# A fourth place for split weights, low splits behind the norms, and a first gate/up step by tile in a four-layer fp32 decoder

## The reference

```python
for i in range(2):                                  # L0, L1
    q, k, v = project_qkv(x, w_qkv[i], cos, sin)    # 16 query heads, 4 key heads of 64, partial rope
    a = moba_attention(q, k, v) if i == 0 else sliding_window_attention(q, k, v, sinks)
    x = layer_norm(alpha * x + a @ w_o[i], ...)
    f = (swiglu(x, w_ffn_gate, w_ffn_up, w_ffn_down) if i == 0        # d_ff 3584
         else moe_swiglu(x, w_router, w_gate, w_up, w_down))         # 8 experts of 3584, top 2
    x = layer_norm(alpha * x + f, ...)
    x = x + (p[i] @ w_ple_proj[i]) * sigmoid(x @ w_ple_gate[i])
for l in range(2):                                  # L2, L3
    h = hybrid_mixer(rmsnorm(x, pre_mix_norm[l]), ...)   # gated delta rule and dilated attention
    x = x + rmsnorm(h, post_mix_norm[l])
    u = causal_conv3(rmsnorm(x, pre_ffn_norm[l]) @ ffn_up[l]) + bias  # 2 x 2816 columns
    x = x + rmsnorm((gelu(gate) * val) @ ffn_down[l], post_ffn_norm[l])
```

## Time and profile before

| | us |
|---|---|
| median of 3 runs | 2222.71 (2221.61 to 2225.2) |
| the profiled execution | 2222.56 |
| its span | 2220.8 |
| TensorE busy | 2165.2 |
| VectorE busy | 1740.5 |
| ScalarE busy | 1423.9 |

### The profile page before, as it was taken

The page is one execution under the profiler, slowest core; times in us unless marked ns, Lnnn a source line. Parts: engine busy times, 40 slices in busy tenths (PEclk is TensorE's granted clock), DMA queues, the critical chain, the costliest instruction groups (busy, mean ns, idle before and its releaser), DMA issues.

```text
span 2220.8 us, 30779 instructions
## 1 busy us (share of the span) xinstructions
PE 2165.2 (97%) x11356; PEld 1808.8 (81%) x11356; DVE 1740.5 (78%) x2003; ACT 1423.9 (64%) x1581; POOL 54.9 (2%) x72
## 2 busy tenths in 40 slices
PE   9999999989999999999999999989999999999998
PEld 6688897668888888888888887779978898987888
DVE  7765567688888888888888889767667886776886
ACT  6544434657877777777777776656565556565654
POOL 2000000010000000000000003000000000000000
PEclk9999999999999999999999999999999999999999
DMA  9755554269999999999999999843135454224551
GB/s 387 261 190 190 190 184 178 105 238 388 367 389 369 393 371 383 371 387 377 366 388 372 386 362 385 338 170 137 67 139 193 177 202 151 81 105 152 190 187 60
DMA packets 83234, 573.25 MB, mean 258 GB/s; under 512 B 9712, under 2 KB 10336, under 8 KB 17936
## 3 DMA queue, kind: packets, MB, share of 16 engines
q1 hardware_dynamic: 77472, 545.29, 64.6%
q0 software_dynamic: 5376, 26.12, 3.2%
q10 hardware_dynamic: 288, 0.52, 0.1%
HBM read 564.03 MB, written 17.83 MB: 262 GB/s over the span
## 4 chain that ended last, share of the span: by engine, by line
PE 85%; DVE 7%; ACT 4%; issue 2%; DMA 1%; SPq 0%; ACTq 0%; DVEq 0%
PE bank L800 63%; PE bank L866 10%; PE bank L868 5%; DVE w_lo L538 2%; ACT w_hi L533 2%; PE bank L1150 1%; PE bank L1275 1%; PE bank L1285 1%; DVE R L2023 1%; PE bank L1190 1%; DVE arena L2034 1%; ACT arena L1483 1%; DMA raw<-in_wu_qkv 1%; ACT L533 0%; PE bank L921 0%
## 5 line engine op out<-in xcount | busy, mean ns | idle before, releaser
L538 DVE TENSOR_TENSOR w_lo<-raw,w_hi 128x2048 fp32r<-128x2048 f32 x505 | 1156.4, 2300 | 263.5 <-ACT w_hi L533 261.8
L533 ACT CAST w_hi<-raw 128x2048 fp32r<-128x2048 f32 x505 | 963.8, 1912 | 351.0 <-PE bank L800 261.3
L800 PE MATMUL bank<-w_hi,xT 128*128 128x512 f32 x2368 | 754.9, 393 | 10.5 <-DVE xT L1978 4.2
L800 PEld LDWEIGHTS bank<-w_hi,xT 128*128 128x128 f32 x2368 | 445.4, 188 | 116.0 <-DVE w_lo L538 11.8
L800 PE MATMUL bank<-w_lo,xT 128*128 128x512 f32 x1184 | 462.0, 390 | 0.0
L800 PE MATMUL bank<-w_hi,aT_hi 128*128 128x512 f32 x864 | 344.0, 398 | 2.4 <-DVE w_lo L538 2.4
L866 PE MATMUL bank<-xT,w_hi 128*128 128x512 f32 x960 | 341.1, 399 | 4.1 <-DVE xT L1978 2.9
L800 PE MATMUL bank<-w_hi,aT_lo 128*128 128x512 f32 x864 | 337.4, 390 | 0.0
L800 PE MATMUL bank<-w_lo,aT_hi 128*128 128x512 f32 x864 | 336.5, 389 | 0.0
L868 PE MATMUL bank<-xT,w_lo 128*128 128x256 f32 x960 | 269.9, 281 | 0.0
L800 PEld LDWEIGHTS bank<-w_lo,xT 128*128 128x128 f32 x1184 | 222.8, 188 | 44.1 <-issue 0.5
(11 more groups left out here) (340 smaller groups left out, 1697.3 us busy)
## 6 DMA issues: line engine op xcount, KB each, us to landing
raw<-in_wu_eg SPq DMA_DIRECT2D x112, 1024.0 KB, 7.2
raw<-in_wu_eu SPq DMA_DIRECT2D x112, 1024.0 KB, 7.2
raw<-in_wu_ed SPq DMA_DIRECT2D x112, 1024.0 KB, 7.3
raw<-in_wu_up SPq DMA_DIRECT2D x44, 1024.0 KB, 4.8
raw<-in_wu_ffn_gu SPq DMA_DIRECT2D x28, 1024.0 KB, 4.8
raw<-in_wu_in SPq DMA_DIRECT2D x28, 1024.0 KB, 4.9
raw<-in_wu_down SPq DMA_DIRECT2D x22, 1024.0 KB, 4.8
raw<-in_wu_ffn_d SPq DMA_DIRECT2D x14, 1024.0 KB, 4.8
```

The costliest lines, as they stand in the source:

```text
L533: nc.scalar.copy(w_hi[:, place(i), :], src).then_inc(*E.hi.mark("unit", i))
L538: nc.vector.tensor_tensor(w_lo[:, place(i), :], raw[:, i % RAW, :], w_hi[:, place(i), :].bitcast(F32), ALU.subtract) \
L800: mm = nc.tensor.matmul(o, l[i], r[j], start=(first and n == 0), stop=(last and n == 2), skip_group_check=not lone)
```

## The change

Outside the experts there are DEEP = 4 places for split units and 4 raw slots; a `walk` there splits the unit four further on. In the experts `vec` and `X` are the fifth and sixth raw slot, so the load into the fifth waits for the tokens' last use of the vectors and the sixth for the dispatch; GpSimd loads the vectors 6 and 7 after the loop. The start of L0 splits unit 3 alone, and the next one ahead of the keys' rope. Low splits that stood ahead of norms stand behind them. In L0, L2 and L3 the first gate/up step is made of `first_high(L, 0)` between the turns of the tiles, `first_high(L, 1)` and `first_low(L)`, and the turned tiles stand in banks 0 to 3.

```diff
-WARM_START, WARM_LN, WARM_RMS = 4, 4, 4
+WARM_START, WARM_LN, WARM_RMS = 4, 4, 2
 RAW = 6
+RAW_OUT = 4
+RAW_OVF = 3
 SPLIT = 3
+DEEP = 4
...
+        raw = [raw_out[:, s, :] for s in range(RAW_OUT)] + [a[:, :, :].rearrange("p a b -> p (a b)") for a in (vec, X)]
+        high = [w_hi[:, s, :] for s in range(DEEP)]
+        low = [w_lo[:, s, :] for s in range(DEEP)]
...
-            return (4 if stage[1] == "mix" else 0) + 2 * t + g
+            return 2 * g + t if stage[1] == "mix" else 2 * t + g
...
+            if base is None:
+                no = split_units.index(i) + DEEP
+                if no < len(split_units) and not i < expert_base <= split_units[no]:
+                    split(E, eng, split_units[no])
+            elif E is M or i + SPLIT < TURN:
+                split(E, eng, i + SPLIT)
...
+                                if j < RAW_OUT:
+                                    sp.wait_ge(*at_once(M.lo, "unit", expert_base - RAW_OUT + j))
+                                if j == RAW_OUT:
+                                    sp.wait_ge(*x_ready.at(1, "mix", 1))
+                                if j == RAW_OUT + 1:
+                                    sp.wait_ge(*xg_put.at("all"))
+                                    sp.wait_ge(*at_once(M.act, "scaled"))
+                                    sp.wait_ge(*at_once(M.groups, "moe", "first", "ga", 1))
...
+                gp.wait_ge(*M.lo.at("unit", expert_base + TURN - 1))
+                load_vec(6)
+                load_vec(7)
...
+            def first_high(L, t):
+
+                for i in range(2):
+                    n = unit_at["gu", L, 0, i]
+                    tile_ready((L, "mix"), t, (i,))
+                    pe.wait_ge(*M.hi.at("unit", key_of(n)))
+                    for half in range(2):
+                        for m in range(2):
+                            b = 4 + 2 * half + m
+                            o = open_bank(M, b) if i == 0 and t == 0 else bank[b]
+                            both = o[:, :].rearrange("p (a n) -> p a n", a=2)[:, :, t * P:(t + 1) * P]
+                            for kc in range(4 * i, 4 * i + 4):
+                                c0 = (kc % 4) * 512 + half * 256 + m * P
+                                nc.tensor.matmul(both, high[place(n)][:, c0:c0 + P], x_both[:, :, kc, t * P:(t + 1) * P],
+                                                 start=(kc == 0 and t == 0), stop=False, skip_group_check=True)
+
+            def first_low(L):
+
+                for i in range(2):
+                    key = ("gu", L, 0, i)
+                    u = unit(M, pe, key)
+                    for half in range(2):
+                        for m in range(2):
+                            for kc in range(4 * i, 4 * i + 4):
+                                c0 = (kc % 4) * 512 + half * 256 + m * P
+                                mm = nc.tensor.matmul(bank[4 + 2 * half + m][:, S:2 * S], u[1][:, c0:c0 + P], xT[0][:, kc, :],
+                                                      start=False, stop=(kc == KC - 1), skip_group_check=True)
+                        if i == 1:
+                            mm.then_inc(*M.groups.mark("gu", L, 0, half))
+                    name = ("gu", L, 0, 1) if i else ("unit",) + key
+                    if i == 0:
+                        mm.then_inc(*M.groups.mark(*name))
+                    released(M, unit_at[key], *name)
...
-                    if s < n - 2:
-                        features(L, s, None if s else (L, "mix"))
+                    if s == 0:
+                        first_high(L, 1)
+                        first_low(L)
+                    elif s < n - 2:
+                        features(L, s)
                     else:
                         o = [open_bank(M, 4 + 2 * (s % 2) + half) for half in range(2)]
...
-                keep_warm(WARM_LN, 6)
+                if L == 0:
+                    first_high(L, 0)
+                else:
+                    keep_warm(WARM_LN, 6)
...
-                keep_warm(WARM_RMS, turn_bank((L, "mix"), 1, 0))
+                keep_warm(WARM_RMS, 6)
+                first_high(L, 0)
                 enter("mix", 1)
...
-                if L:
-                    walk("qkv", L, 4)
+                walk("qkv", L, 4)
                 block(2, 4)
...
-            walk("qkv", 0, 4)
+            nc.scalar.copy(high[place(2)][:, half:UNIT], raw[2][:, half:UNIT]).then_inc(*M.hi.mark("unit", 2))
...
-                walk("wo", L, 0)
-                walk("wo", L, 2)
+                if L == 0:
+                    walk("wo", L, 0)
+                    walk("wo", L, 2)
+                else:
+                    for i in range(2):
+                        split_hi(M, ac, expert_base + i)
                 norm_root(L, "mix", 0)
-                walk("wo", L, 1)
+                if L == 0:
+                    walk("wo", L, 1)
                 copy_T((L, "mix"), L, 0)
-                walk("wo", L, 3)
+                if L == 0:
+                    walk("wo", L, 3)
                 norm_root(L, "mix", 1)
                 copy_T((L, "mix"), L, 1)
                 if L == 0:
...
                 walk("wo", L, 0)
                 want_root()
                 half_squares(L, "mix", 0, wo_halves)
+                sum_squares(L, "pre", 0, x_ready.at(L, "mix", 0))
                 walk("wo", L, 2)
-                sum_squares(L, "pre", 0, x_ready.at(L, "mix", 0))
                 walk("wo", L, 1)
                 half_squares(L, "mix", 1, wo_halves)
+                copy_T((L, "mix"), L, 0)
                 sum_squares(L, "pre", 1, x_ready.at(L, "mix", 1))
-                for t in range(NT):
-                    copy_T((L, "mix"), L, t)
+                copy_T((L, "mix"), L, 1)
                 walk("wo", L, 3)
                 dense_act(L)
                 n = FFN_STEPS[L]
...
-                walk("wo", L, 0)
+                if L == 0:
+                    walk("wo", L, 0)
+                else:
+                    split_lo(M, ve, expert_base)
                 half_stats(0, 0, take_wo)
-                walk("wo", L, 2)
                 half_stats(0, 1, take_wo)
                 tile_normed(L, "mix", 4 * L, 0)
-                norm_tile(L, "mix", 4 * L, 1, take_wo)
-                for t in range(NT):
+                half_stats(1, 0, take_wo)
+                if L == 0:
+                    rest_T((L, "mix"), L, 0)
+                half_stats(1, 1, take_wo)
+                tile_normed(L, "mix", 4 * L, 1)
+                for t in range(1 if L == 0 else 0, NT):
                     rest_T((L, "mix"), L, t)
-                walk("wo", L, 1)
-                walk("wo", L, 3)
                 if L == 0:
+                    walk("wo", L, 2)
+                    walk("wo", L, 1)
+                    walk("wo", L, 3)
                     dense_dve(0)
                     for t in range(NT):
                         norm_tile(L, "ffn", 4 * L + 2, t, take_y)
                     rest_T((L, "ffn"), L, 0)
+                    rest_T((L, "ffn"), L, 1)
                     walk("dn", 0, FFN_STEPS[0] - 2)
-                    rest_T((L, "ffn"), L, 1)
                     walk("dn", 0, FFN_STEPS[0] - 1)
                 else:
-                    split_lo(M, ve, expert_base)
                     route()
                     select(M, "moe", "first", 0, 0)
                     rows_and_gates()
...
             def enter_mix(L):
+                post_products(L, "mix", 4 + 2 * L, 1, wo_halves)
                 pre_turned(L, "mix", 0)
+                post_residual(L, "mix", 1, wo_halves)
+                rest_T((L, "mix"), L, 0)
                 pre_scale(L, "mix", "pre", 1)
-                rest_T((L, "mix"), L, 0)
                 pre_turned(L, "mix", 1)
                 rest_T((L, "mix"), L, 1)
             for L in range(2, 4):
                 if L == 2:
...
                 post_tile(L, "mix", 4 + 2 * L, 0, wo_halves)
+                pre_scale(L, "mix", "pre", 0)
+                enter_mix(L)
                 walk("wo", L, 2)
-                pre_scale(L, "mix", "pre", 0)
-                post_tile(L, "mix", 4 + 2 * L, 1, wo_halves)
-                enter_mix(L)
                 walk("wo", L, 1)
                 walk("wo", L, 3)
                 dense_dve(L)
...
                 if L == 2:
                     rest_T((3, "in"), 3, 0, (1,))
-                    walk("dn", L, n - 2)
                     pre_scale(3, "in", "in", 1)
                     pre_turned(3, "in", 1)
                     rest_T((3, "in"), 3, 1)
+                    walk("dn", L, n - 2)
                     walk("dn", L, n - 1)
```

More of the change, by code:

```diff
@@ L512, in unit @@
             pe.wait_ge(*E.lo.at("unit", key_of(i)))
-            return w_hi[:, place(i), :], w_lo[:, place(i), :]
+            return high[place(i, E)], low[place(i, E)]
         def released(E, i, *key):
@@ L527, in split_hi @@
             src = wait_loaded(E, ac, i)
-            back = i - SPLIT - (1 if any(i - SPLIT <= w < i for w in whole) else 0)
```

(30 more changed lines are left out.)

134 lines of the change are left out of this document (80 added, 54 removed).

## The result

The changed kernel takes 2235.35 us (median of 5 runs, 2234.24 to 2237.07) against 2222.71: 1.005 times the time before (95% interval 1.0039 to 1.006), +12.6 us. The profiled execution took 2237.00, span 2235.2; before it was 2222.56, so the trace accounts for +14.4.

What follows compares the result with a forecast made beforehand. TensorE, busy 2165.2 of 2220.8 us, was taken to bound the kernel. Terms +1.95 - 1.0 - 0.85 + 0.3 + 8.4 - 1.05 + 1.6 = +9.35 us on 2222.56 (median 2222.71) gave 2232.0, range 2219 to 2238.

Steps and rivals of the forecast that it cites:

- the wait in L2 and L3: Before step 1, TensorE idles about 2.7 us until VectorE's sum, held behind four low splits, frees bank 4.
- rival D: Experts: the first loads starve TensorE, forecast +6 us, 2238; chance 0.07.
- rival E: Outside the experts: four raw slots hold the stream back, the four places stay unfilled, ScalarE waits for loads; 2237; chance 0.06.
- L0's start: Extra pair of splits ahead of the keys' rope delays the first scores from 43.19 to 45.15: +1.95 us.
- the clock: New idle times at three places, L0, L2 and L3, bring one drop of the granted clock: +1.6 us, bounds 0 and +5.
- L2 and L3 as a whole: First gate/up step by tile in L2 and L3: +4.2 us each, bounds +1.7 and +5.8; the largest term.
- The idle time ahead of tile 0's piece: L2 and L3: warm-up lasts only 1.8 us, so TensorE idles about 2.3 us before tile 0's piece.
- the late bank 6: L2, step 1: the second sum, 3.67 us behind the first, opens bank 6 at 1677.4 against 1673.20, +4.2 us.
- L0's first step: L0's first gate/up step by tile: the step after starts at 111.25 against 112.24, -1.0 us; bounds -3.8 and +0.7.
- The attention of L0: From L0's first scores to the turn of tile 0: the softmax sets the pace, no further shift, 0.
- L1, L2 to L3, experts: L1 loses low-split waits, -0.85 us; a low split moves behind between L2 and L3, -1.05; experts' later loads, +0.3.
- Rival B: L0, L2, L3: banks come free in time because the low splits fit earlier gaps; 2222.6 us, no change; chance 0.20.

Runs made afterwards that it cites:

- experiment 1: Changed kernel with the sums ahead of the down unit's split in each dense feed-forward's first step; 2227.27 us, ratio 1.0014.
- 7: Kernel before, three places and six raw slots, with only L0's first step by tile, sums first; 2223.75 us, ratio 0.9997.
- 8: As 7, and between L2 and L3 the low split of the next to last down unit behind tile 1's xT; 2228.95 us, ratio 1.0025.
- 9: Kernel before with SP's loads outside the experts held to four ahead, as four raw slots would make it; 2228.45 us, ratio 1.0017.
- 2: Changed kernel with the first gate/up step whole again in L0, L2 and L3, norm orders left as changed; 2230.30 us, ratio 1.0029.
- 4: Changed kernel with GpSimd's fills of the experts' rows moved behind L0's norm (about 345 us); 2241.60 us, ratio 1.0086.
- 5: Changed kernel with sums ahead of the down unit's split and GpSimd's fills right behind L0's attention; 2230.84 us, ratio 1.0032.
- 6: As 5, with L2's and L3's first step whole and their norm order as before the change; 2229.34 us, ratio 1.0021.
- 10: Changed kernel with four warm-up matmuls instead of two ahead of tile 0's piece in L2 and L3; 2233.60 us, ratio 1.0042.
- 12: As 11, with the extra high split of L0's start ahead of the angles' sine on ScalarE; 2218.34 us, ratio 0.9976.
- 3: Changed kernel with the extra split of L0's start behind the keys' rope instead of ahead of it; 2237.72 us, ratio 1.0064.
- 11: Changed kernel with sums ahead of the down unit's split, L2's and L3's first step whole and norm order as before; 2224.07 us, ratio 0.9999.

## Why the prediction was right, and where not

Forecast 2232.0 in 2219 to 2238, measured 2235.35: 3.4 over. What carried the forecast, the wait in L2 and L3, was right. That 2235 lies inside the range is partly luck: the range reached up to 2238 for rivals D and E, which did not come, and what filled it, L0's start and the clock, was not foreseen at that size.

- *L0, L2 and L3, the wait ahead of step 1* (2.75 each predicted, 2.89 measured): right in place, size and cause, shown by experiment 1. L2 and L3 as a whole: 4.64 and 4.46 for 4.2, with a fall of the clock in each that stood in another term; to the start of step 1 the shift in L2 is +3.42, for 3.6. Two details were off and cancel. The idle time ahead of tile 0's piece was 1.72, not 2.3. And the late bank 6, +0.6 in the sum, did not show: the clock fell behind the wait, the first 8 pairs, granted 0.50 for the most part, took until 1686.3, and bank 6 was free at 1685.4; the fall cost instead.
- *L0's first step* (-1.0): +1.17. To the start of step 1 it was -0.6; then the clock fell behind the 2.89, +1.7 (short by that much from 110 to 130).
- *L0's start* (+1.95, bounds 0 and +2.7): the step of the sum that failed. The mechanism is there, and its size can be told apart from the start's own spread: from the high split of unit 3 to the first scores the kernels without the extra split (before, 7, 8, 9) take 24.9 to 25.0, those with it and the load in time (2, 4, 5, 6, 10) take 26.6 to 26.7, and 12, with its high split in ScalarE's wait, 25.0. So the extra split costs 1.6, for 1.95; the terms named for it (2.74 less a wait of 0.5) would give 2.2, and the working does not say where the rest went. Missing was a second wait, 2.44 for the third wo unit, which makes the 29.1 of the changed kernel (L0's row of the table, +4.11) and lies outside my bounds. I had put the four raw slots into rival E and set it low because "outside the experts the queue is far from full"; at L0's start it is full (DMA share 1.02 from 20 to 40 us in the kernel before), and there they told, together with the extra split (9, 12). That the fills hold the load up fits 4, 5 and 6, where it was in time in all three, but it was so in 2 and 10 as well, so their share is not settled.
- *The attention of L0* (0): +1.96, a fall of the clock around waits of 1.32 and 2.30 (1.23 and 0.72 in the kernel before). A wait of 2.3 or more there and the fall (granted 0.52 to 0.83 in the window from 50) came in all four kernels with the late load (the changed one, 1, 3, 11), and in none where it was in time (2, 4, 5, 6, 10, 12), where the waits are 1.2 and 0.72.
- *L1, L2 to L3, experts* (-0.85, -1.05, +0.3): -1.30, -1.10, -0.23. The experts' fifth and sixth slots cost nothing; rival D did not come.
- *Clock* (+1.6 for one fall): under-counted. The 1.6 is what the 20 us at 0.92 in the earlier trace rows are short of 1.00; a fall behind the 2.89 is short by 1.7 here. The runs give an estimate of 5.8 us in all, the profile falls at 52, 118, 1486, 1530, 1682 and 2054 in place of 100 and 1891, and is short by 5.1 between 1440 and 1470, where the kernel before was short by 3.4 (1430 to 1460). I took one fall for the three places, because the clock had fallen behind idle 1.20, turn, idle 1.08 and had not behind turn, idle 1.45; the trace has one fall at each of the three. What they share is the wait of 2.89: experiment 1 has the same turns and as few warm-up matmuls, with 0.40 in place of the 2.89, and its clock falls at none of the three. The two places I had set beside each other are not alike either: the turn of L0 is 8 matmuls at L777 and took 1.10, that of L2 16 through a diagonal at L775 and took 2.05. The fall at L2's entry stays unexplained: the idle time there is the same 2.40 as before the change, where the clock did not fall behind it (1480.42). Why it fell there in the changed kernel and in nine of the twelve experiments' profiles is open.
- *Rival B* would have needed the sums in front; the kernel that has them (1) came to +3.9, not 0. Its L2 lost 1.4, close to the 1.7 that B gave; L0's start, late by 4 us there, is what B did not have.

## What to carry to other kernels

When a pipeline of look-ahead work is made one deeper, every place where the look-ahead stands in program order means another unit: check at each what now waits behind it, above all ahead of the instruction that frees an accumulator (2.89 us of wait ahead of step 1 here). Memory for one more split place taken from the load ring moves requests later (from 17.24 to 30.21 for one unit here); at the start, where the DMA share was 1.04 from 20 to 40 us, ScalarE then waited 2.44 for it ahead of the first scores. And put an extra split where its engine already waits (12: +4.1 became 0), before judging whether the deeper pipeline pays.

## What the runs showed that was not expected

- Execution times of one kernel spread by up to 11 us here (the kernel before 2219.47 to 2227.69 over 28 runs, e11 2218.3 to 2229.13), and the granted clock goes from 0.992 to 0.997 in the 28 and from 0.990 to 0.996 in e11: a step of 1 to 2 us shows in a profile and not in ten runs' median (7).
- The granted clock fell to 0.50 (windows of 0.5 us) behind 2.89 us of wait following 7.9 us of matmuls of 256 columns at 11 of the 12 places that had that wait (three each in the changed kernel and in 3, 4 and 10; not in L0 in 4). Behind the 2.40 at L2's entry it did not in the kernel before (1.00 from 1480 to 1490), and did in nine of the twelve experiments' profiles (0.83 in e1_sums_first).
- Moving 19 transfers of 512 KB off the start brought waits of 4.3 to 8.4 us wherever else they were put in L0 (4, 5, 6): from 25 us on they run beside an attention that needs few weights (in the kernel before SP asks for three units between 44 and 91 us).
